# Decoder step with paged attention: keys turned on VectorE in 32x32 blocks, scores in four row bands, two tokens of a page in each partition

## Chip, cores and metric

One Trainium2 chip, one core. The metric is the device time of one execution in microseconds (us), lower is better.

## What is computed

One step of a one-layer decoder for a prompt of 256 tokens and 8 sample sequences of 8 new tokens each: feed-forward, mixer (paged attention and a gated linear state, side by side), feed-forward, each with a conditioned scale, shift and gate. All is fp32. The part around the change is the attention of the sample sequences over their paged past of 2048 tokens, 16 pages of 128 tokens, 8 heads of 64:

```python
k_past = cache_k[layer, page_table].reshape(B, past, H, HD)
kmean = jnp.mean(k_past[:, :own0].reshape(B, n_full, MOBA_BLOCK, H, HD), axis=2)
idx, ok = moba_select(q, kmean, n_full)          # top 3 of 8 blocks of 256 tokens, per query and head
...
s_sel = jnp.einsum('bqhd,bhqnkd->bqhnk', q, k_sel) * scale
s_sel = jnp.where(ok[..., None], s_sel, -jnp.inf).reshape(B, H, T, -1)
...
o = sparse_softmax_attend(s_sel, v_sel, s_own, v_own)
```

## The kernel before

The activations stand as [128 partitions = channel, 8 channel tiles, 320 tokens]: 256 prompt and 64 sample columns. Weights stream through four raw slots of 8 KB a partition; ScalarE rounds each to a high part (`wh`), VectorE subtracts for the low part (`wl`), and TensorE makes three products (L691, L692, L696). The slots are numbered: conditioning and first feed-forward, the mixer's input projection MI (74 to 85), its output projection MO (86 to 89), second feed-forward.

**The page stage** lies between MI and MO. The 8 sequences are taken as 4 pairs `i`, with `bi` the member of the pair. A page is 256 KB in K and as much in V; four pages make a group of 1 MB, so there are 32 K groups and 32 V groups. Each is loaded by `load_pages` on SyncE's queue: four DMAs of one page, token per partition, 2 KB a packet (L619), in the written order `PAGE_GROUPS`. `place_groups` gives each group a buffer: four in `ring` (over the raw slots), and for parts of the stage places in `Hh`/`Hl`, in `M` and in `W`. SyncE waits with each group until the last user of its buffer is done (`wait_used`).

For each K group `turn_keys(i, j, bi)` makes 16 transposes on TensorE (L887), one PSUM bank of four for each page; ScalarE (`keys_act`) or VectorE (`keys_dve`, L1785) copies each bank to `kT`. `scores(i, j)` (L898) then multiplies for both members and four head pairs `c`: stationary `Qz` (128 x 32, zeros where another head stands), moving 512 tokens of `kT`, each product in its own 32 columns of the array, so that four lie side by side, in bank `B[j % 2]`. VectorE reduces the bank twice, sum for the choice of blocks and maximum (`block_values`, L1792 and L1794), ScalarE copies it to `prob` (`scores_out`).

After four `j` VectorE's `choose` (L1812 to L1823) ranks the blocks and makes the biases; ScalarE takes the exps (`exps`), TensorE turns the probabilities (`turn_probs`, L918), both engines copy them to `PT`, and `values(i, bi)` (L936, own tokens L941) multiplies with V as it landed, in PSUM bank 2. `own_heads` (VectorE, L1849), `pick_heads` (TensorE, L950), `out_high` and `out_low` move the result to the input of MO.

**What sets the order.** Every engine's order is written out by hand. Between these steps stand the mixing steps `mix(k)`, placed by `point(x)` and the table `AT_POINT`: 0 to 6 are the prompt's own attention (per head on VectorE L1864 to L1877), 12 to 15 the output and norm of the gated linear part (L1011 to L1035), 16 to 19 the new sample states (TensorE L1053, VectorE L1965). What TensorE fills in PSUM in this stage (turned keys, mixing results, own scores, turned probabilities, picked heads) rotates over banks 3 to 7 in the written order `FILLS`; `turn_bank` waits until the engine that reads the bank's former content is done. Engines run each its own list in order, so whatever waits holds all that stands behind it.

`turn_keys` and `scores` of before:

```python
for p in range(4):
    bank = turn_bank(("k", i, j, bi, p))
    for c in range(HP):
        m = pe.transpose(bank[:, c * P:(c + 1) * P], at[p][:, c * P:(c + 1) * P], ident)
```
```python
m = pe.matmul(B[j % 2][32 * c:32 * c + 32, :], Qz[:, 2 * i + bi, c, :], kT[:, bi, c, :],
              start=(bi == 0), stop=(bi == 1))
```

Of the kernel before, what the change touches and what calls it, by code (L numbers as in the profile page):

```python
# [21 lines left out]
F32 = mybir.dt.float32  # L22
# [38 lines left out]
GROUPS = RING // 4  # L61
# [76 lines left out]
def key_fills(i, j):  # L138

    return [("k", i, j, bi, p) for bi in range(2) for p in range(4)]  # L140


PAGE_GROUPS = [("k", 0, j, bi) for j in range(4) for bi in range(2)]
# [6 lines left out]
for _lv in range(6):  # L150
    GAPS[6 + _lv] += mix_fills(7 + _lv)
GAPS[8] += [("nv", t) for t in range(3)]
# [3 lines left out]
AT_POINT = {0: 0, 1: 1, 3: 2, 4: 3, 5: 4, 6: 5, 8: 6, 9: 12, 10: 13, 11: 14, 13: 15, 14: 16, 15: 17, 16: 18, 18: 19}  # L156
# [5 lines left out]


FILLS += key_fills(0, 0) + key_fills(0, 1) + point_fills(0) + key_fills(0, 2) + point_fills(1) + [("own", 0)]
FILLS += key_fills(0, 3) + point_fills(2)
for _i in range(NPAIR):
    _m = 5 * _i + 3
    if _i + 1 < NPAIR:
        PAGE_GROUPS += [("k", _i + 1, j, bi) for j in range(2) for bi in range(2)]
        FILLS += key_fills(_i + 1, 0) + point_fills(_m) + key_fills(_i + 1, 1) + point_fills(_m + 1)  # L170
    else:
        FILLS += point_fills(_m)
    PAGE_GROUPS += [("v", _i, g, 0) for g in range(4)]
    if _i + 1 < NPAIR:
        PAGE_GROUPS += [("k", _i + 1, 2, bi) for bi in range(2)]
    PAGE_GROUPS += [("v", _i, g, 1) for g in range(4)]
    FILLS += [("p", _i, q) for q in range(5)]
    if _i + 1 < NPAIR:
        PAGE_GROUPS += [("k", _i + 1, 3, bi) for bi in range(2)]
        FILLS += point_fills(_m + 2) + key_fills(_i + 1, 2) + point_fills(_m + 3) + [("own", _i + 1)]  # L180
        FILLS += key_fills(_i + 1, 3) + point_fills(_m + 4) + [("pick", _i)]
    else:
        FILLS += point_fills(_m + 1) + [("pick", _i)]
GROUP_AT = {key: n for n, key in enumerate(PAGE_GROUPS)}
FILL_AT = {key: n for n, key in enumerate(FILLS)}
IN_RING, IN_H, IN_M, IN_W = range(GROUPS), GROUPS, GROUPS + 1, GROUPS + 2
BEGIN_AT = {GROUP_AT[("v", 1, 0, 0)]: IN_M, GROUP_AT[("v", 2, 0, 0)]: IN_W}
LAST_IN = {IN_H: GROUP_AT[("v", 2, 3, 0)], IN_M: GROUP_AT[("k", 3, 3, 1)], IN_W: GROUP_AT[("v", 3, 0, 0)]}


def place_groups():

    queue, last, buf, before = [(MI + x) % R for x in range(R)] + [IN_H], {}, [], []
    for n in range(len(PAGE_GROUPS)):
        if n in BEGIN_AT:
            queue.insert(0, BEGIN_AT[n])
        queue = [b for b in queue if n <= LAST_IN.get(b, n)]
        b = queue.pop(0)
        queue.append(b)
        buf.append(b)  # L200
        before.append(last.get(b))
        last[b] = n
    return buf, before, last
# [4 lines left out]
BANK = [4 + n % 4 if n < IN_MI else 3 + (n - IN_MI) % 5 for n in range(len(FILLS))]  # L208
# [3 lines left out]
def on_act(key):  # L212

    if key[0] == "k":
        _, i, j, bi, p = key
        if j == 0:
            return i == 0 or p != 3
        return p % 2 == 0 if j >= 2 else (bi == 1 and p % 2 == 1)
    if key[0] == "p":
        return key[2] in (2, 3)  # L220
    if key[0] == "ga":
        return key[1] == 5
    return key[0] in ("rg", "nk", "nv", "nvg", "pt", "kd", "sp")
# [17 lines left out]
def shape_constants():  # L241
# [24 lines left out]
    parts["cos"], parts["sin"] = cos, sin  # L266
    q = p[:, None]
# [16 lines left out]
    reset = np.ones((P, N))  # L284
    reset[:, [0] + [S + T * b for b in range(NB)]] = 0.0
    parts["reset"] = reset
# [26 lines left out]
def layer_kernel(nc, a, o):  # L313
    ctx = ExitStack()
    with ctx:
# [17 lines left out]
        ring = sb("ring", [P, RING, 512])  # L333
        kT = sb("kT", [P, 2, HP, 512])
# [24 lines left out]
        Qz = sb("Qz", [P, NB, HP, 32])  # L359
# [20 lines left out]
        B = [ctx.enter_context(nc.psum_tensor(f"B{i}", [P, 512], F32)) for i in range(8)]  # L380
        OB = 2
# [13 lines left out]
        def raw_view(n):  # L395

            if n == MO:
                return M[:, :, :].rearrange("p c n -> p (c n)")[:, 0:SLOT]
            return W[:, 0:SLOT] if n == MO + 1 else raw[:, n % R, :]
# [5 lines left out]
        def page_at(b, j):  # L405
# [4 lines left out]
            if b == IN_M:  # L410
                return M[:, :, :].rearrange("p c n -> p (c n)")[:, 512 * j:512 * j + 512]
            if b == IN_W:
                return W[:, 512 * j:512 * j + 512]
            return ring[:, 4 * b + j, :]

# [42 lines left out]
        gmask = C("gmask").rearrange("p (l i) -> p l i", l=5)  # L458

# [3 lines left out]
        page_landed = [sem(f"page_landed_{i}") for i in range(GROUPS + 3)]  # L463
# [26 lines left out]
        tp_filled, tp_act, tp_dve = sem("tp_filled"), sem("tp_act"), sem("tp_dve")  # L490
        s_out, own_ready, bias_ready, exp_done = sem("s_out"), sem("own_ready"), sem("bias_ready"), sem("exp_done")
        rinv_ready, v_used, pv_out, om_ready = sem("rinv_ready"), sem("v_used"), sem("pv_out"), sem("om_ready")
        o_hi, s_act, s_dve = sem("o_hi"), sem("s_act"), sem("s_dve")
# [184 lines left out]
        def _(pe):  # L678
# [211 lines left out]
            def scores(i, j):  # L890

                if 4 * i + j >= 2:
                    pe.wait_ge(s_act, 4 * i + j - 1)
# [1376 lines left out]
```

## Time and profile before

| | |
|---|---|
| median of 3 runs | 982.14 us (980.75 to 983.33) |
| profiled execution, its own time | 983.45 us |
| its span, first to last instruction | 981.3 us |
| TensorE matmul busy | 919.1 us (94%), 6991 instructions |
| TensorE weight load busy (beside the matmuls) | 798.8 us |
| VectorE, ScalarE, GpSimd busy | 545.9, 359.5, 28.1 us |
| HBM read | 195.00 MB, 203 GB/s over the span |
| chain that ended last | TensorE 83%, VectorE 6%, ScalarE 3%, SyncE's queue 3% |

The profile is one execution. "Busy" is the time in which an engine had an instruction in work; for TensorE the trace keeps two records for each fp32 product and one for a transpose. The page's second part cuts the span in 40 slices of 24.5 us. PEclk is the granted TensorE clock as a share of 2.4 GHz, and the DMA share is the mean busy share of the core's 16 DMA engines, which can read a little over 1 where packets overlap.

### The profile page before, as it was taken

To read this page: it belongs to the slowest core of one execution; us is meant where nothing else is said; L and a number is where in the kernel's file an instruction comes from. 1 tells how busy PE (TensorE), PEld (TensorE's weight loads), DVE (VectorE), ACT (ScalarE), POOL (GpSimd) and SP (SyncE) were. 2 spreads that over 40 slices of the span, in tenths; PEclk is the share of its full clock that TensorE was granted. 3 is DMA by queue.
4 is the path that set the end of the run, shared out by engine and by line. 5 is a ranking of instruction groups with operands and counts; after the bars stand their busy time and mean duration, and the time that the engine had idled before them with its cause. 6 is when DMAs were issued, how large, how long until landed. Compare 5 with 4: busy or idle time off the path is not lost.

```text
span 981.3 us, 17319 instructions
## 1 busy us (share of the span) xinstructions
PE 919.1 (94%) x6991; PEld 798.8 (81%) x6991; DVE 545.9 (56%) x839; ACT 359.5 (37%) x509; POOL 28.1 (3%) x34
## 2 busy tenths in 40 slices
PE   6999999999999899999878999859899999989997
PEld 2588888988999599996665877548779999989994
DVE  0545444454655677785843538443666765554655
ACT  1424322232442534454642426240333232323433
POOL 0000000000000000000000000001200000000000
PEclk9999999998999999999999889877999999999999
DMA  9899889886456744448858998996416465534511
GB/s 329 258 299 258 240 244 257 245 235 169 127 152 191 256 129 145 144 153 268 297 190 325 324 325 310 356 343 199 125 39 167 133 163 139 145 89 122 155 50 53
DMA packets 214885, 199.93 MB, mean 204 GB/s; under 512 B 9569, under 2 KB 161261, under 8 KB 214678
## 3 DMA queue, kind: packets, MB, share of 16 engines
q1 hardware_dynamic: 213412, 194.99, 64.8%
q0 software_dynamic: 704, 2.49, 0.7%
q10 hardware_dynamic: 690, 1.35, 0.4%
q8 instruction: 55, 0.90, 0.4%
q14 instruction: 24, 0.20, 0.1%
HBM read 195.00 MB, written 3.80 MB: 203 GB/s over the span
## 4 chain that ended last, share of the span: by engine, by line
PE 83%; DVE 6%; ACT 3%; SPq 3%; issue 2%; DMA 2%; ACTq 0%; DVEq 0%
PE B L691 20%; PE B L692 19%; PE B L696 19%; PE B L751 4%; PE B L887 3%; PE B L898 2%; SPq L619 2%; PE B L936 2%; PE B L775 2%; PE B L760 2%; PE B L791 2%; DMA ring<-in_cache_v 1%; PE B L1017 1%; PE B L717 1%; PE B L712 1%
## 5 line engine op out<-in xcount | busy, mean ns | idle before, releaser
L691 PE MATMUL B<-Hh,wh 128*128 128x320 f32 x912 | 274.2, 314 | 0.6 <-issue 0.6
L692 PE MATMUL B<-Hl,wh 128*128 128x320 f32 x912 | 270.5, 310 | 0.0
L1595 DVE TENSOR_TENSOR wl<-raw,wh 128x2048 fp32r<-128x2048 f32 x90 | 207.3, 2305 | 94.3 <-ACT wh L1240 94.0
L1240 ACT ACTIVATE wh<-raw 128x2048 fp32r<-128x2048 f32 x90 | 172.3, 1914 | 150.3 <-PE B L696 117.6
L691 PEld LDWEIGHTS B<-Hh,wh 128*128 128x128 f32 x912 | 172.4, 189 | 10.7 <-issue 10.0
L692 PEld LDWEIGHTS B<-Hl,wh 128*128 128x128 f32 x912 | 172.4, 189 | 0.3
L696 PE MATMUL B<-Hh,wl 128*128 128x320 f32 x912 | 152.8, 310 | 0.0
L696 PEld LDWEIGHTS B<-Hh,wl 128*128 128x128 f32 x912 | 139.1, 189 | 0.0
L691 PE MATMUL B<-Gh,wh 128*128 128x320 f32 x352 | 107.1, 317 | 2.5 <-DVE Gl L1721 2.5
L692 PE MATMUL B<-Gl,wh 128*128 128x320 f32 x352 | 106.7, 316 | 0.0
L1240 ACT ACTIVATE sg<-B 128x320 f32<-128x320 f32 x46 | 20.1, 438 | 210.1 <-PE B L696 195.7
L1713 DVE TENSOR_TENSOR hf<-sg,B 128x320 f32<-128x320 f32 x44 | 21.5, 488 | 124.6 <-ACT sg L1240 124.6
L691 PEld LDWEIGHTS B<-Gh,wh 128*128 128x128 f32 x352 | 68.5, 195 | 2.7 <-DVE Gl L1721 2.7
L692 PEld LDWEIGHTS B<-Gl,wh 128*128 128x128 f32 x352 | 68.6, 195 | 0.0
L887 PE MATMUL B<-cst,ring 128*128 128x128 f32 x432 | 53.2, 277 | 7.0 <-DVE kT L1785 1.8
L887 PEld LDWEIGHTS B<-cst,ring 128*128 128x128 f32 x432 | 47.1, 141 | 14.4 <-issue 6.4
L696 PE MATMUL B<-Gh,wl 128*128 128x320 f32 x352 | 56.8, 309 | 0.0
L696 PEld LDWEIGHTS B<-Gh,wl 128*128 128x128 f32 x352 | 53.1, 188 | 0.0
L1785 DVE COPY kT<-B 128x512 f32<-128x512 f32 x62 | 40.2, 686 | 21.9 <-PE B L887 21.5
L1240 ACT ACTIVATE kT<-B 128x512 f32<-128x512 f32 x66 | 36.0, 611 | 24.4 <-PE B L887 24.3
L936 PE MATMUL B<-ring,PT 128*32 128x128 f32 x672 | 26.0, 308 | 14.3 <-DMA ring<-in_cache_v 14.3
L751 PE MATMUL B<-raw,cpk 128*32 128x512 f32 x288 | 38.8, 617 | 0.3 <-ACT cpk L1240 0.3
(246 smaller groups left out, 951.8 us busy)
## 6 DMA issues: line engine op xcount, KB each, us to landing
raw<-in_w_ffn_in SPq DMA_DIRECT2D x88, 512.0 KB, 6.2
raw<-in_w_ada SPq DMA_DIRECT2D x72, 512.0 KB, 4.9
ring<-in_cache_k SPq DMA_DIRECT2D x108, 256.0 KB, 5.3
ring<-in_cache_v SPq DMA_DIRECT2D x84, 256.0 KB, 5.0
raw<-in_w_ffn_out SPq DMA_DIRECT2D x32, 384.0 KB, 3.6
raw<-in_w_mix_in SPq DMA_DIRECT2D x24, 512.0 KB, 4.7
raw<-in_w_ffn_out SPq DMA_DIRECT2D x32, 320.0 KB, 4.3
M<-in_cache_v SPq DMA_DIRECT2D x16, 256.0 KB, 4.5
```

The source lines that it names most:

```text
L619: sp.dma_start(page_at(b, j), cache[bass.ds(page[j], 1), :, :].rearrange("o s f -> s (o f)")).then_inc(page_landed[b], 16)
L691: pe.matmul(out, w, xh[k], start=start and k == 0, stop=False)
L692: pe.matmul(out, w, xl[k], start=False, stop=False)
L696: m = pe.matmul(out, w, xh[k], start=False, stop=stop and k == last)
L751: m = pe.matmul(B[4 + pair % 2][32 * k:32 * k + 32, :], cpk[:, 4 * half + k, :], v[:, k, :], start=(half == 0), stop=(half == 1))
L760: m = pe.matmul(B[bank][:, col:col + NC], arow[:, h // 2, h % 2 * P:(h % 2 + 1) * P], C("comb"), start=True, stop=True)
L887: m = pe.transpose(bank[:, c * P:(c + 1) * P], at[p][:, c * P:(c + 1) * P], ident)
L936: m = pe.matmul(out[32 * c:32 * c + 32, :], PT[:, 4 * g + p, 32 * c:32 * c + 32], at[p][:, c * P:(c + 1) * P], start=(g == 0 and p == 0), ...
L1240: return act.activation(out, in_, func, **kw)
L1595: dve.tensor_tensor(wl[:, wbuf(n), :], raw_view(n), f32(wh[:, wbuf(n), :]), ALU.subtract).then_inc(lo_ready, 1)
L1713: step(dve.tensor_tensor(hf[:, j, :], sg[:, j, :], B[2 * j][:, 0:N], ALU.mult))
L1785: dve.tensor_copy(kT[:, bi, :, p * P:(p + 1) * P], tb(key).rearrange("p (c s) -> p c s", c=HP)).then_inc(tp_dve, 1)
```

## The change

- K pages are turned on VectorE: one in-place `transpose` for a group, 128 x 2048, which turns each 32x32 block within itself. `kT`, the key transposes and the key copies go.
- A page lands two tokens to a partition (64 partitions, 4 KB a packet), K and V alike; two pages fill 128 partitions. Each page is still one DMA.
- Scores take the turned blocks in four bands of 32 rows (`a`): a chunk is two K groups of one member (8 pages) and 64 products of 32 rows, 32 columns and 256 moving columns; 16 chunks in all. The four bands write four PSUM banks, `S4` (over banks 0 to 3).
- The queries are turned to fit (`turn_queries`, 8 calls of 16 products), ScalarE copies them to `Qs`.
- ScalarE copies a band set in 4 pieces and sums each block on the way (`accum_out`); VectorE takes only the maximum (`block_max`), from `prob` in SBUF.
- Six ring groups of 1 MB instead of four, and other late places; value products use bank 4; the fills rotate over banks 5 to 7 instead of 3 to 7. `Qz` lies over constants that are dead by then and is cleared later, after the rotary step.
- Mixing steps move to other points; the turned probabilities' first quarter is copied by ScalarE.

The diff, cut to its core:

```diff
-GROUPS = RING // 4
+GROUPS = 6
...
+AT_POINT = {x: x if x <= 6 else x + 5 for x in range(15)}
...
+USE = [key for s in range(2) for bi in range(2) for key in key_groups(0, s, bi)]
+FILLS += point_fills(0) + point_fills(1) + [("own", 0), ("q", 1, 0)] + point_fills(2) + [("q", 1, 1)]
+    for _x in range(3):
+        FILLS += point_fills(4 * _i + 3 + _x)
+    FILLS += [("p", _i, q) for q in range(5)] + point_fills(4 * _i + 6)
+        USE += key_groups(_i + 1, 0, 0) + key_groups(_i + 1, 0, 1) + value_groups(_i, 0)
+        USE += key_groups(_i + 1, 1, 0) + value_groups(_i, 1) + key_groups(_i + 1, 1, 1)
+        FILLS += [("q", _i + 2, 0)] if _i + 2 < NPAIR else []
+        FILLS += [("own", _i + 1)]
+        FILLS += [("q", _i + 2, 1)] if _i + 2 < NPAIR else []
+        USE += value_groups(_i, 0) + value_groups(_i, 1)
+    FILLS += [("pick", _i)]
+PAGE_GROUPS = [key for key in USE if key != ("v", 0, 0, 0)]
+PAGE_GROUPS.insert(6, ("v", 0, 0, 0))
...
-BANK = [4 + n % 4 if n < IN_MI else 3 + (n - IN_MI) % 5 for n in range(len(FILLS))]
+BANK = [4 + n % 4 if n < IN_MI else 5 + (n - IN_MI) % 3 for n in range(len(FILLS))]
...
-                    sp.dma_start(page_at(b, j), cache[bass.ds(page[j], 1), :, :].rearrange("o s f -> s (o f)")
+                    sp.dma_start(page_pair_at(b, j // 2)[64 * (j % 2):64 * (j % 2) + 64, :],
+                                 cache[bass.ds(page[j], 1), :, :].rearrange("o (s x) f -> s (o x f)", x=2)
                                  ).then_inc(page_landed[b], 16)
...
+            def turn_queries(i, bi):
+
+                bank = turn_bank(("q", i, bi))
+                if i == 0:
+                    pe.wait_ge(q_ready, 4)
+                for x in range(4):
+                    for q in range(4):
+                        m = pe.matmul(bank[32 * q:32 * q + 32, P * x:P * (x + 1)], ident[:, 32 * x:32 * x + 32],
+                                      Qz[:, 2 * i + bi, :, :].rearrange("p c r -> p (c r)"), start=True, stop=True)
+                m.then_inc(tp_filled, 1)
+
+            def scores(i, s, bi):
+
+                if bi == 0 and 2 * i + s >= 1:
+                    pe.wait_ge(s_act, 2 * i + s)
+                if s == 0:
+                    wait_act(("q", i, bi))
+                pe.wait_ge(k_turned, 2 * chunk(i, s, bi) + 2)
+                b = BUF[GROUP_AT[("k", i, 2 * s, bi)]]
+                for x in range(4):
+                    for a in range(4):
+                        for c in range(HP):
+                            f = P * c + 32 * x
+                            m = pe.matmul(S4[32 * c:32 * c + 32, a, 0:256].rearrange("r (p j) -> r p j", p=8),
+                                          Qs[32 * a:32 * a + 32, bi, x, c, :],
+                                          ring[32 * a:32 * a + 32, 4 * b:4 * b + 8, f:f + 32],
+                                          start=(bi == 0 and x == 0), stop=(bi == 1 and x == 3))
+                m.then_inc(s_out, 1)
...
+            scores(0, 0, 0)
             point(0)
+            scores(0, 0, 1)
             point(1)
             own_scores(0)
+            scores(0, 1, 0)
+            turn_queries(1, 0)
             point(2)
+            scores(0, 1, 1)
+            turn_queries(1, 1)
             for i in range(NPAIR):
+                m0 = 4 * i + 3
                 if i + 1 < NPAIR:
                     point(m0)
+                    scores(i + 1, 0, 0)
                     point(m0 + 1)
+                    scores(i + 1, 0, 1)
+                    point(m0 + 2)
                     turn_probs(i)
                     values(i, 0)
                     point(m0 + 3)
+                    scores(i + 1, 1, 0)
+                    if i + 2 < NPAIR:
+                        turn_queries(i + 2, 0)
                     values(i, 1)
                     own_scores(i + 1)
+                    scores(i + 1, 1, 1)
+                    if i + 2 < NPAIR:
+                        turn_queries(i + 2, 1)
                     pick_heads(i)
                 else:
                     turn_probs(i)
                     values(i, 0)
                     values(i, 1)
                     pick_heads(i)
...
+            def queries_out(i, bi):
+
+                wait_fill(("q", i, bi))
+                if i >= 1:
+                    act.wait_ge(s_out, chunk(i - 1, 1, bi) + 1)
+                act_(Qs[:, bi, :, :, :].rearrange("p x c r -> p (x c r)"), tb(("q", i, bi))).then_inc(tp_act, 1)
+
+            def scores_out(i, s):
+
+                act.wait_ge(s_out, chunk(i, s, 1) + 1)
                 if i >= 1:
                     wait_fill(("p", i - 1, 4))
+                for m in range(4):
+                    n = 4 * s + m
+                    last = act_(prob[:, BLK * n:BLK * (n + 1)].rearrange("p (a j x) -> p a x j", a=4, x=2),
+                                S4[:, :, 64 * m:64 * m + 64].rearrange("p a (x j) -> p a x j", x=2),
+                                accum_out=gate[:, n:n + 1])
+                last.then_inc(s_act, 1)
...
+            def turn_keys(i, s, bi):
+
+                for g in (2 * s, 2 * s + 1):
+                    n = GROUP_AT[("k", i, g, bi)]
+                    b = BUF[n]
+                    dve.wait_ge(page_landed[b], 64 * TURN_IN[n])
+                    v = ring[:, 4 * b:4 * b + 4, :].rearrange("p j f -> p (j f)")
+                    dve.transpose(out=v, in_=v).then_inc(k_turned, 1)
+
+            def block_max(i, s):
+
+                dve.wait_ge(s_act, 2 * i + s + 1)
+                dve.tensor_reduce(bmax[:, 4 * s:4 * s + 4],
+                                  prob[:, 4 * BLK * s:4 * BLK * (s + 1)].rearrange("p (n k) -> p n k", n=4), X_AXIS,
+                                  ALU.max).then_inc(dve_step, 1)
                 step.k += 1
...
+                if n >= 10:
+                    turn_keys(0, 0, n - 10)
 
             def point(x):
                 if x in AT_POINT:
                     mix(AT_POINT[x])
 
             point(0)
+            turn_keys(0, 1, 0)
             point(1)
+            block_max(0, 0)
             own(0)
+            turn_keys(0, 1, 1)
             point(2)
             for i in range(NPAIR):
+                m0 = 4 * i + 3
+                block_max(i, 1)
+                choose(i)
                 if i >= 1:
                     out_low(i - 1)
                 if i + 1 < NPAIR:
+                    turn_keys(i + 1, 0, 0)
                     point(m0)
+                    turn_keys(i + 1, 0, 1)
                     point(m0 + 1)
+                    point(m0 + 2)
+                    totals(i)
                     probs_dve(i, 1)
+                    probs_dve(i, 4)
+                    point(m0 + 3)
+                    block_max(i + 1, 0)
+                    turn_keys(i + 1, 1, 0)
+                    own_heads(i)
+                    own(i + 1)
+                    turn_keys(i + 1, 1, 1)
+                else:
                     totals(i)
+                    probs_dve(i, 1)
                     probs_dve(i, 4)
                     low(At(MO))
                     own_heads(i)
                     out_low(i)
```

## Rows read from the trace of the kernel before

**Rows 1.** The page, second part: rate in each of 40 slices.

```profile
GB/s 329 258 299 258 240 244 257 245 235 169 127 152 191 256 129 145 144 153 268 297 190 325 324 325 310 356 343 199 125 39 167 133 163 139 145 89 122 155 50 53
```

**Rows 2.** Windows: length, PE, PEld, DVE, ACT, POOL busy, PEclk, DMA share, GB/s.

```profile
482.00:533.00 51.00, 39.09 (x526) 28.90 (x519) 25.68 (x67) 20.02 (x60) 0.00 (x0) 0.93 0.77 270
533.00:588.00 55.00, 53.73 (x622) 44.17 (x621) 25.26 (x55) 19.84 (x49) 0.00 (x0) 0.88 0.88 305
...
638.00:670.00 32.00, 19.25 (x305) 15.11 (x305) 12.07 (x31) 10.18 (x25) 1.18 (x1) 0.66 0.95 320
sum 223.00, PE 188.53 PEld 142.62 DVE 118.09 ACT 93.35 POOL 1.90; mean PE 37.71 PEld 28.52 DVE 23.62 ACT 18.67 POOL 0.38
```

**Rows 3.** Groups by form, 447 to 670 us: busy, mean ns | idle before, releaser.

```profile
L887 PE MATMUL B<-cst,ring 128*128 128x128 f32 x432 | 53.2, 277 | 7.0 <-DVE kT L1785 1.8 <-DMA ring<-in_cache_k 1.7 <-DVE arow L1801 1.6
...
L1785 DVE COPY kT<-B 128x512 f32<-128x512 f32 x62 | 40.2, 686 | 21.9 <-PE B L887 21.5
...
L898 PE MATMUL B<-kT,Qz 128*32 128x512 f32 x256 | 33.7, 640 | 0.1
...
L1240 ACT ACTIVATE prob<-prob,small 128x256 f32<-128x256 f32 x32 | 15.9, 507 | 4.0 <-DVE small L1823 4.0
L1792 DVE TENSOR_REDUCE small<-B 128x2 f32<-128x512 f32 x16 | 11.0, 688 | 43.4 <-PE B L898 43.4
```

**Rows 4.** Waits of SyncE's DMA queue: total us, times, longest.

```profile
SPq L619 <- PE B L936: 33.6, 5, 10.8
```

**Rows 5.** Timeline and L906's source view, TensorE: start, us, records.

```profile
464.90 1.92 PE L898 MATMUL B<-kT,Qz 128*32 128x512 f32 x16
466.64 0.41 PE L906 MATMUL B<-knew,Qz 128*32 128x64 f32 x16
...
574.59 1.94 PE L936 MATMUL B<-M,PT 128*32 128x128 f32 x32
578.23 1.04 PE L936 MATMUL B<-ring,PT 128*32 128x128 f32 x32
...
L906 PE MATMUL B<-knew,Qz x64: 219/219/220, 466.6 to 631.8; 128*32 128x64 f32 x64
```

**Rows 6.** Page, fifth part, and source view of L1902: VectorE within SBUF.

```profile
L1595 DVE TENSOR_TENSOR wl<-raw,wh 128x2048 fp32r<-128x2048 f32 x90 | 207.3, 2305 | 94.3 <-ACT wh L1240 94.0
...
L1902 DVE TENSOR_SCALAR Z<-Z x5: 427/427/428, 400.0 to 435.7; 128x512 f32<-128x512 f32 x5
```

**Rows 7.** Timeline of VectorE: choice of blocks, prompt mixing, state update.

```profile
479.66 0.21 DVE L1812 TENSOR_TENSOR small<-small 128x64 f32<-128x64 f32 x1
...
482.00 0.56 DVE L1864 TENSOR_TENSOR Z<-B,cst 128x384 f32<-128x384 f32 x1
...
485.95 3.67 DVE L1785 COPY kT<-B 128x512 f32<-128x512 f32 x6
...
601.73 1.23 DVE L1965 SCALAR_TENSOR_TENSOR W<-W,rstd,B 64x128 f32<-64x128 f32 x4
```

**Rows 8.** Timeline of TensorE: first rows of mixing 13, values, mixing 14.

```profile
548.24 0.46 PE L1011 MATMUL B<-W 128*128 128x128 f32 x2 [1.11 <-issue]
...
555.14 1.93 PE L936 MATMUL B<-M,PT 128*32 128x128 f32 x32
...
564.69 0.39 PE L1011 MATMUL B<-W 128*128 128x128 f32 x2
```

**Rows 9.** Windows of one microsecond, columns as in rows 2.

```profile
522.00:523.00 1.00, 1.00 (x28) 0.99 (x24) 0.00 (x0) 0.00 (x0) 0.00 (x0) 0.53 1.05 389
16.00:17.00 1.00, 1.00 (x7) 0.24 (x9) 0.00 (x0) 0.00 (x0) 0.00 (x0) 1.00 1.06 422
```

**Rows 10.** Timeline of the stage's end: last choice, values, output projection.

```profile
642.18 0.23 DVE L1823 TENSOR_SCALAR small<-small 128x8 f32<-128x8 f32 x1
...
647.87 1.29 PE L936 MATMUL B<-W,PT 128*32 128x128 f32 x32
...
670.02 0.61 PE L691 MATMUL B<-Hh,wh 128*128 128x320 f32 x1 [0.62 <-issue]
```

## Prediction before the run

> **What bounds the kernel now.** The change touches one stage, so I first read the rates by fortieths of the span, to find it: from slice 18 on the rate stands near 325 GB/s for ten slices and falls to 39 right after [rows 1]. Those are the 64 MB of K and V pages. The windows of that stage then say who fills it. Of 223 us TensorE is busy 188.5, VectorE 118.1 and ScalarE 93.4, and even the transfers' share falls to 0.77 in one stretch [rows 2]. Nothing is saturated throughout: TensorE leads from 533 to 588 us, and from 638 to 670 us it is busy only 19 of 32. The costliest groups show what TensorE does for the keys: 432 of the 512 transposes on ring tiles take 53.2 us, the scores 33.7 us, and VectorE copies the turned keys out of PSUM for 40.2 us, with reductions of 11 us each for sum and maximum [rows 3]. Last, SyncE's own waits: it stood 33.6 us for the value products to free a buffer before it could issue the next pages [rows 4]. So the bound alternates: TensorE's instructions, then pages issued late because the ring was full.
>
> **What the change removes.** (a) TensorE's 512 key transposes. Sixteen take about 1.92 us in a stream, so 61 us. (b) The old scores, 16 calls of 1.92 us [rows 5], less the overlap at their ends: 28 us. (c) On VectorE 62 key copies (40.2 us) and 32 reductions out of PSUM (22 us) [rows 3]. (d) The key copies on ScalarE, which has room [rows 2]; its new copies of the scores (four pieces of 256 columns, 2.2 us by the 0.5 us that one exp of 256 columns takes here [rows 3]) are shorter than what they replace.
>
> **What it adds.** (e) VectorE turns 32 key groups of 128x2048 in place. No transpose stands in the trace. From above, four copies of 512 columns out of PSUM would be 2.7 us, and the subtraction of the same 128x2048 takes 2.305 us with two inputs. From below, a one-input instruction of 512 elements within SBUF took 0.427 us; four of them are 1.7 us, and nearly half of each is a fixed part (an instruction of 64 elements takes 0.21), so 0.43 + 3 x 0.25 = 1.2 us for 2048 [rows 3, 6, 7]. I take 2.2 us, near the subtraction, because that is the row of the same size and a transpose is no plain pass; 4.4 us for the two groups that one score chunk needs, 70 us in all.
> (f) Scores in bands: 16 chunks of 64 fp32 products (32 rows, 32 columns, 256 moving), which the trace counts twice each, as it does the old ones: 128 records. The row nearest in kind is the own-key score, 16 records of 64 moving columns in 0.41 us, of which 0.22 is the length of one: 13 ns apart [rows 5]. With four times the columns but four times as many products side by side the array needs the same 13 ns: 1.9 us a chunk. That is the lower bound. A long stream, the value products, held 27.5 ns a record (32 in 0.88 and the latency) [rows 5]: 3.7 us. If the four bands do not run beside one another, four records share 0.215 us (half of the 0.43 us of the 512-column ones): 7.0 us. At the lower clock level, 1.2 GHz, the array's own times double: the first bound becomes 3.6 us. The clock follows how full TensorE is: mean 0.88 where it was busy 53.7 of 55 us, 0.66 where it was busy 19.3 of 32, and 0.53 at 522 us, so practically the lower level, behind a wait for pages [rows 2, 9]; 32 value records then take 1.94 us, at full clock 1.04 [rows 5]. Most chunks will start behind 4 to 5 us of waiting for VectorE's turning, so I take 3.6 us.
> A rule of the Trainium skill speaks against the change here: "TensorEngine Tiling (Array Packing)", section Performance Considerations, has about 60 cycles of overhead in each matmul. By it a chunk would need 3.2 us at full clock and 6.4 at half, and the sum would end 28 us later. The own-key row, at 13 ns a record, does not show that overhead, so its case is a rival (R4) and not the forecast.
> (g) The queries are turned in 8 calls of 32 records, at 27.5 ns 0.9 us each. Two sit in the projection loop, where TensorE is never idle: 1.8 us straight onto the path.
> (h) Packets of 4 KB instead of 2 KB. The page stream peaks near 388 GB/s; in the one microsecond where the 4 KB rows of x_prompt arrive the rate is 422 [rows 9]. Worth at most 8% of a transfer that only matters where it is waited for. I cost it at nothing in the middle: pages wait for buffers there. The DMA count and SyncE's issue work do not change.
> (i) More buffers (six ring groups, three more late): the last pages need no longer wait for values. Today the last choice of blocks ends at 642.4 us, the values start 5.4 us later and wait for pages, and the output projection starts at 670.0 [rows 10]: 27.6 us. With the pages landed these remain: 5.4 us, values of 4.9 us (32 records at the low clock) and 3.7, and 2.4 of head picking, 16.4 us. This is the surest gain, 11 us.
>
> **The path.** The order on VectorE is written out by hand, and a turn waits behind what stands ahead of it. The turn for the third chunk of each pair stands behind the mixing step that follows the first values; the one for the fourth stands behind own_heads, which waits for the second values. So turning is not hidden: turn, scores, values, turn, scores come one after the other. Before, TensorE could turn keys while anything else was late. I follow it from row durations: choice of blocks 2.3 us (479.66 to 482.00), a prompt mixing step on VectorE 4.0 (482.00 to 485.95), two sample-state updates with their masks 3.2 (1.23 for one's four instructions) [rows 7], copy of scores 2.2 plus a maximum of 1.2; mixing step 13 on TensorE 6.9 (548.24 to 555.14) and 14 9.9 (564.69 to 574.59) [rows 5, 8], with 6.5 taken for the first since its opening gap of issue goes.
> Pair 0, from 447.0 us: turns 13.2, mixing, maximum and own keys 8.5, scores 3.6, copy, maximum and choice 5.7: choice 0 ends at 478 us (today 482.0).
> Pair 1: turns 4 x 4.4, scores 3 x 3.6 (one is hidden), mixing 3 and 6 with maxima 7.3, mixing 5 and turned probabilities 3.5, queries 0.9, values 2 x 3.9, own heads 1.1, copy and choice 5.7: 54.8, choice 1 at 532.8.
> Pair 2: turns 3 x 4.4 (one lies beside mixing 13), scores 4 x 3.6, mixing 13 to 15 19.0, probabilities 2, values 4.9 and 4.2, maximum, queries, own heads, remainders 3.7, copy and choice 5.7: 67.1, choice 2 at 599.9.
> Pair 3: turns 4 x 4.4, updates 3.2, 4.7 and 3.2, probabilities and values behind them 4.2, mixing 19 with maximum 6.3, scores 2 x 3.6, values 4.2, own heads and rest 1.3, copy and choice 5.7: 57.6, choice 3 at 657.5 (today 642.4).
> Tail 16.4: 673.9. Plus the 1.8 us of (g): the output projection starts at 675.7, today at 670.0. That is 5.7 us more. Behind it nothing changes. The profiled execution took 983.45 us (span 981.3), 1.3 above the median of the runs, 982.14; 983.45 and 5.7 make 989.2, on the median's scale **988 us**. A measurement of this kernel tells 0.3%, some 3 us, from no change. The terms that decide are 14 exposed pairs of turns (62 us) and 10 exposed chunks (36 us), 98 together, against the 89 us of transposes and scores that TensorE loses; the 11 us of (i) stand on the other side.
>
> **Rivals.** R1, scores are quick: TensorE stays at 2.4 GHz and 13 ns a record hold, chunk 1.9 us. For it: the own-key row. Against it: the idle time ahead of the chunks. 10 x 1.7 off: 971. Chance 0.22.
> R2, VectorE turns at its faster one-input rate, 1.2 us a group. For it the 0.427 us row, against it that such a turn crosses partitions. 28 x 1.0 off: 960. Chance 0.07.
> R3, the transfers alone set the end, as the larger packets intend. 60 groups and two weight slots, 65 MB, remain at 446.7; at 388 to 422 GB/s they are in by 614 to 601, and the projection starts 4 us later: 917 to 930. It needs TensorE and VectorE hidden behind them, and TensorE alone needs 188 - 89 + 52 + 6 = 157 us. Chance 0.05.
> R4, slower beyond my forecast: the bands bring no more than four products side by side, because their row groups do not overlap or because each record has a floor of its own. Place: each chunk. Price: 7.0 us, or the 54 ns a record of the values at the low clock, 6.9, against 3.6: 10 x 3.4 = 34, so 1022. It turns a tie into a loss from about 4 us a chunk on. Chance 0.13. The skill's 60 cycles above would end here as well.
> R5, a turn costs twice my value, 4.4 us a group: 28 x 2.2 = 62: 1050. Chance 0.05.
> R6, the change does not free TensorE as it says: three rotating PSUM banks instead of five make it wait for copies. Two of the five probability fills a pair then wait for a copy of 0.69 us and its hop of 0.2: 4 x 2 x 0.9 = 7 us, 995. Chance 0.08.
>
> **How the numbers follow.** The forecast has 0.40, with 978 to 998 as its own spread (ten hops of 0.2 us a pair that I did not count push up, warm chunks push down). Faster by over 0.3%: R1 to R3, 0.34, and 0.03 of the forecast's own spread: 0.37. Same, 979.2 to 985.1: 0.15 of that spread. Slower: the rest, 0.48. Range 955 to 1018: it leaves out R3, the near-zero end of R2, R5 and the far half of R4, some 0.2.
>
> **What would show it.** Right: transposes near 2.2 us on VectorE with TensorE idle ahead of each chunk, released by VectorE; chunk times near 3.6 us at clock 0.5; values no longer waiting for pages; choice 1 earlier than today, choice 3 later. Wrong: chunks under 2.5 us; transposes under 1.5; a page stream at 400 GB/s without gaps, which would mean that the chain of turns was hidden after all.

## The result and the profile after

The changed kernel took 1075.88 us (median, 1071.58 to 1078.92), the kernel before 981.44 us on the same chip (978.08 to 983.33): 1.096 times as long, 95% interval 1.091 to 1.102. Forecast were 988 us and a range of 955 to 1018. The sign of the forecast stands, its size doesn't: 94 us were lost, not 6. The profiled execution took 1078.92 us (span 1076.8). Medians and intervals here are of runs in the faster of the chip's two states, which leaves out two of four runs of e3 and one each of e6 and e10 below; the traces of e3 and e10 are of such slower runs.

The page of the kernel after, second and third parts (compare the rates with [rows 1]):

```profile
PEclk9999999989999999977666777566789999999998
DMA  9898898874567345796999899999751555533521
GB/s 333 251 307 252 239 249 239 238 199 115 155 216 250 109 154 136 166 250 166 213 224 241 188 217 206 224 212 237 199 137 40 154 143 144 146 108 108 161 56 49
...
q1 hardware_dynamic: 197028, 194.99, 68.6%
```

Three windows of the kernel after (length, PE, PEld, DVE, ACT, POOL busy, PEclk, DMA share, GB/s):

```profile
450.00:470.00 20.00, 12.58 (x356) 7.08 (x347) 16.53 (x30) 4.72 (x17) 0.00 (x0) 0.75 1.04 232
510.00:530.00 20.00, 10.47 (x231) 8.62 (x231) 6.94 (x6) 3.65 (x13) 0.00 (x0) 0.70 1.05 229
710.00:730.00 20.00, 6.89 (x139) 4.76 (x140) 8.07 (x14) 4.38 (x20) 0.00 (x0) 0.65 1.06 242
```

Read the last two columns together. The DMA engines are full (1.04 to 1.06) and move 229 to 242 GB/s. The kernel before moved 389 with engines just as full [rows 9]. The transfers themselves have become slow: from issue to landing a page of keys for the ring takes 7.6 us (median), before 5.3, and a page of values 11.0, before 5.0. The stage now ends at 764.05 us, before at 670.0 [rows 10], so practically the whole loss lies in it.

Groups of the kernel after, 447 to 766 us (busy, mean ns | idle before, releaser), the transposes from the page, then waits of SyncE's queue and of TensorE in the same stretch:

```profile
L940 PE MATMUL S<-ring,Qs 32*32 32x256 f32 x2048 | 70.8, 573 | 85.5 <-DVE ring L1805 62.5 <-issue 21.6 <-DVE M L2080 1.4
L1810 DVE TENSOR_REDUCE small<-prob 128x4 f32<-128x1024 f32 x8 | 9.7, 1214 | 24.5 <-ACT prob L1277 24.5
```

```profile
L1805 DVE STREAM_TRANSPOSE ring<-ring 128x2048 f32<-128x2048 f32 x32 | 72.4, 2292 | 11.8 <-DMA ring<-in_cache_k 11.7
```

```profile
SPq L654 <- PE S L940: 91.0, 13, 17.2
```

```profile
PE S L940 <- DVE ring L1805: 62.5, 11, 9.8
PE S L940 <- issue: 21.6, 7, 4.8
PE B L984 <- DMA ring<-in_cache_v: 12.3, 3, 7.6
```

A turn takes 2.29 us. TensorE stands 62.5 us for turns; the forecast's 62 were 14 waits of 4.4, these are 11, some of them with a late page of keys in them, so that the two sums agree is in part luck. SyncE's queue stands 91.0 us for score products (L940), because keys stay in the ring until they are scored. Before, it stood 33.6 us for values [rows 4] and little for keys:

```profile
SPq L619 <- PE B L887: 12.6, 8, 2.4
```

Chunks and tail, timeline of TensorE after:

```profile
504.89 2.75 PE L940 MATMUL S<-ring,Qs 32*32 32x256 f32 x128 [2.22 <-DVE ring L1805]
568.63 4.31 PE L940 MATMUL S<-ring,Qs 32*32 32x256 f32 x128 [8.31 <-DVE ring L1805]
...
746.32 1.94 PE L984 MATMUL B<-ring,PT 128*32 128x128 f32 x32 [7.55 <-DMA ring<-in_cache_v]
...
764.05 0.60 PE L727 MATMUL B<-Hh,wh 128*128 128x320 f32 x1 [0.62 <-issue]
```

These two chunks take 2.75 us, behind a wait of 2.2 (granted clock 1.00, the level of 2.4 GHz), and 4.31 behind one of 8.3 (0.54, close to the level of 1.2 GHz). The last choice ends at 727.3 us, and 37 us pass to the output projection, since the last values wait for pages.

### The profile page after: what moved, and what is told of

It reads as the page before. It is cut to its first block, busy times and chain, and to the rows that moved or that the text cites. A ratio compares the mean times of both kernels' runs of the same rounds, so it can differ in the third digit from the quotient of the medians.

```text
span 1076.8 us, 20151 instructions
## 1 busy us (share of the span) xinstructions
PE 920.8 (86%) x8527; PEld 798.6 (74%) x8527; DVE 565.7 (53%) x781; ACT 335.0 (31%) x503; POOL 28.0 (3%) x34
## 3 DMA queue, kind: packets, MB, share of 16 engines
q1 hardware_dynamic: 197028, 194.99, 68.6%
## 4 chain that ended last, share of the span: by engine, by line
PE 77%; DVE 10%; issue 5%; DMA 4%; SPq 2%; ACT 2%; ACTq 0%; DVEq 0%
PE B L727 18%; PE B L728 17%; PE B L732 17%; PE S L940 5%; DVE ring L1805 5%; PE B L787 3%; SPq L654 2%; PE B L984 2%; PE B L811 2%; PE B L827 2%; PE B L796 2%; DMA ring<-in_cache_v 2%; DMA ring<-in_cache_k 2%; PE B L1065 1%; DVE small L1810 1%
## 5 line engine op out<-in xcount | busy, mean ns | idle before, releaser
L940 PE MATMUL S<-ring,Qs 32*32 32x256 f32 x2048 | 70.8, 573 | 85.5 <-DVE ring L1805 62.5
L940 PEld LDWEIGHTS S<-ring,Qs 32*32 32x32 f32 x2048 | 41.8, 130 | 107.3 <-issue 72.4
L1805 DVE STREAM_TRANSPOSE ring<-ring 128x2048 f32<-128x2048 f32 x32 | 72.4, 2292 | 11.8 <-DMA ring<-in_cache_k 11.7
L1277 ACT ACTIVATE prob<-S 128x256 f32<-128x256 f32 x32 | 12.1, 412 | 103.9 <-PE S L940 103.9
```

The lines of the kernel that those rows point to most:

```text
L940: m = pe.matmul(S4[32 * c:32 * c + 32, a, 0:256].rearrange("r (p j) -> r p j", p=8), Qs[32 * a:32 * a + 32, bi, x, c, :], ring[32 * a:32 * ...
L1277: return act.activation(out, in_, func, **kw)
L1805: dve.transpose(out=v, in_=v).then_inc(k_turned, 1)
```

## The experiments

The theories were: **T1**, a transfer that lands on half of the partitions is slow; **T2**, rows of 4 KB are slow; **T3**, the engines stretch the stage and the stream follows. A softmax does not mind the order of its keys, so keys and values of a block may lie on any partitions, if both lie alike. That makes the layout free to vary.

### Where a page lands

e1 and e2 alter the changed kernel, e3 and e4 the kernel before:

```diff
-  sp.dma_start(page_pair_at(b, j // 2)[64 * (j % 2):64 * (j % 2) + 64, :], <two tokens a row, 4 KB>)
+  sp.dma_start(page_pair_at(b, j // 2)[:, 512 * (j % 2):512 * (j % 2) + 512], <one token a row, 2 KB>)   # e1
+  sp.dma_start(page_pair_at(b, j // 2)[j % 2::2, :], <two tokens a row, 4 KB>)                           # e2
-  sp.dma_start(page_at(b, j), <one token a row, 2 KB>)
+  sp.dma_start(page_pair_at(b, j // 2)[64 * (j % 2):64 * (j % 2) + 64, :], <two tokens a row>)           # e3
+  sp.dma_start(page_pair_at(b, j // 2)[j % 2::2, :], <two tokens a row>)                                 # e4
```

> The changed kernel with each page again on all 128 partitions in rows of 2 KB; everything else of the change stays (bands, turn on VectorE, order). T1 (a transfer that lands in 64 partitions is slow): the page stream is back near 388 GB/s and the kernel takes 980 to 1000 us, what the forecast's serial path gives. T2 (rows of 4 KB are slow as such): the same. T3 (the work on VectorE and TensorE stretches the stage and the stream only follows): 1060 to 1080 us, stream 230 to 250 GB/s.

> The changed kernel with its rows of 4 KB, but a page's 64 rows go to every second partition of the 128 instead of one half. T1 in the form that a half is slow because it is one contiguous half: as the run with 2 KB rows, 980 to 1000 us. T1 in the form that 64 rows are too few: 1060 to 1080 us. T2: 1060 to 1080 us. T3: 1060 to 1080 us.

> The kernel before with the changed kernel's page transfers alone: two tokens of a page in each partition, a page in 64 partitions, rows of 4 KB. T1 and T2: the stream falls to 230 to 250 GB/s with nothing else changed, and the kernel takes 1050 to 1090 us. T3: 975 to 990 us, as before.

> The kernel before with rows of 4 KB on every second partition. T1 (contiguous half): 960 to 985 us, at most a little faster than before. T1 (too few rows) and T2: 1050 to 1090 us. T3: 975 to 990 us.

Measured, against 980.34 us for the kernel before: e1 1019.21 (ratio 1.035 to 1.044), e2 1017.85 (1.034 to 1.044), e3 1016.94 (1.030 to 1.045, mean of 1011.83 and 1022.05; all four runs scatter up to 1038.52), e4 979.66 (0.997 to 1.003). e4 came in as T1's narrow form expects. e1 and e2 lie between their expectations, and e3 between 990 and 1050: the layout costs time in both kernels, but less than its theory said. The stretch 520 to 535 us of e3, and the same slices of the pages of e3 and e4:

```profile
520.00:535.00 15.00, 6.73 (x108) 4.92 (x112) 0.00 (x0) 0.00 (x0) 0.00 (x0) 0.57 1.05 229
...
GB/s 332 258 298 248 244 244 244 243 206 154 154 179 275 131 126 149 144 210 247 215 229 236 239 260 272 258 270 224 189 90 82 150 138 160 151 89 119 156 57 51
```

```profile
GB/s 327 259 300 257 239 252 253 244 232 181 120 149 201 258 129 131 155 156 261 291 167 339 305 325 345 299 357 251 128 50 166 132 167 134 145 89 124 157 47 54
```

e3 has not one transpose on VectorE, and for these 15 us VectorE and ScalarE do nothing at all; its engines still read 1.05 at 229 GB/s. So it is not the work of VectorE and ScalarE that slows the stream. e4 has the same 197,028 packets of 4 KB and streams at the old rate. T1 stands in its narrow form: neighbouring partitions, not few rows or long ones. T2 and T3 fall as causes of the slow stream. The changed kernel lies 94 us over the kernel before of its own chip, e2 38, so the layout costs some 57 us here; in the kernel before it costs 37 (31 and 42 in the two runs). Some 38 us remain, for which T3's kind of cause is needed.

### Turn, clock and chunk

All on e2, which from here on is the base. e5 moves the turns on VectorE, e6 leaves all but 32 columns of each out, e7 fills TensorE's waits, e8 and e12 leave half of the score products out:

```diff
+  turn_keys(i + 1, 0, 0)          # e5, ahead of block_max(i, 1) and choose(i)
   block_max(i, 1); choose(i)
-  turn_keys(i + 1, 0, 0)
+  turn_keys(i + 1, 0, 1)
   point(m0)
-  turn_keys(i + 1, 0, 1)
   ...
+  turn_keys(i + 1, 1, 0)
   point(m0 + 3); block_max(i + 1, 0)
-  turn_keys(i + 1, 1, 0)
+  turn_keys(i + 1, 1, 1)
   own_heads(i); own(i + 1)
-  turn_keys(i + 1, 1, 1)
```

```diff
-  dve.transpose(out=v, in_=v)                                    # e6
+  dve.transpose(out=v[:, 0:32], in_=v[:, 0:32])
+  for _ in range(10): pe.matmul(<free columns>, ident, ident)    # e7, before nine chunks
   pe.wait_ge(k_turned, 2 * chunk(i, s, bi) + 2)
-  for x in range(4):                                             # e8, e12
+  for x in range(2):
```

> The changed kernel with 4 KB rows on every second partition (1018 us) and VectorE's order altered: the turns of each of the next pair's four chunks stand one place earlier, ahead of the maxima, the copy of the own columns or the heads they stood behind. Ta (what is left over before is the turn standing in line before each chunk, 60.9 us of TensorE's idle time): 990 to 1005 us. Tb (TensorE's low clock stretches the chunks): 1010 to 1020 us. Tc (the buffers of K, held until the scores, starve the stream in the middle, and its last 40 pages come after the last chunk): 1005 to 1015 us, since an earlier turn frees a buffer earlier.

> The same kernel with the turn on VectorE left out but for 32 columns of each group (32 turns of 2.29 us go, the scores are of unturned keys). Ta: all that the stage lost and more comes back, 955 to 980 us. Tb: 1000 to 1015 us. Tc: 975 to 995 us, where the stream becomes the limit.

> The same kernel with ten idle products of 128x128 on TensorE before nine of the sixteen chunks, in the time in which it waits for the turn (2.2 us at the full clock, results unused). Tb (chunks of 4.3 us at the half clock against 2.75): the granted clock of the stage rises from 0.75 to over 0.85 and 10 to 20 us come back, 998 to 1008 us. Ta and Tc: 1012 to 1025 us.

> The same kernel with half of each chunk's score products left out (64 of 128; two of the four quarters of a head's rows). If the chunk's length is what is exposed (16 of 4.2 us, of which half goes, and half of the stalls named issue): 985 to 995 us. If only the turn is (Ta alone): 1005 to 1015 us.

> Every second partition, the turns early (994.6 us) and the ten idle products before nine chunks (alone 9 us of gain) together. If the two gains add, 984 to 988 us, still not under the kernel before. If the idle products filled just the wait that the early turns have since removed, 993 to 998 us.

> The changed kernel as it is (pages on halves of the partitions, 1076 us) with the early turns alone. If the slow stream sets the stage, the early turns are worth less here than the 23 us that they gave with the full stream: 1062 to 1076 us. If turn and stream cost independently of each other: 1050 to 1056 us.

> Every second partition, the turns early (994.6 us), and half of each chunk's score products left out. If the 15 us that are left over before are the length of the chunks on TensorE: 976 to 984 us. If they are the stream, which starts late because a page of keys holds its buffer until it is scored: 984 to 992 us, since a shorter chunk frees the buffer sooner by 1.3 to 2 us only.

| | us | ratio to before, 95% | us over before, same chip | from | of its expectations |
|---|---|---|---|---|---|
| e5 turns early | 994.60 | 1.012 to 1.021 | 15.8 | e2 1017.85 (37.5 over) | Ta |
| e6 no turns | 984.61 | 1.001 to 1.009 | 5.8 | e2 | Tc |
| e7 idle products | 1008.96 | 1.025 to 1.041 | 30.1 | e2 | just over Tb |
| e8 half of the products | 1002.95 | 1.021 to 1.031 | 24.1 | e2 | between the two |
| e9 = e5 + e7 | 1004.01 | 1.017 to 1.027 | 21.9 | e5 | neither, 6 us over the higher |
| e11 after + e5's order | 1052.73 | 1.068 to 1.080 | 70.6 | after 1075.88 (94.4 over) | independent |
| e12 = e5 + e8 | 986.49 | 1.004 to 1.009 | 4.7 | e5 | the stream |

The runs were made on several chips, so a difference between two kernels is best read from the fourth column.

Groups of e2 (440 to 710 us), then of e5 (440 to 700):

```profile
L940 PE MATMUL S<-ring,Qs 32*32 32x256 f32 x2048 | 66.9, 553 | 66.7 <-DVE ring L1805 60.9 <-issue 4.3 <-DVE M L2080 1.4
```

```profile
L1805 DVE STREAM_TRANSPOSE ring<-ring 128x2048 f32<-128x2048 f32 x32 | 72.7, 2296 | 38.0 <-DMA ring<-in_cache_k 37.9
L940 PE MATMUL S<-ring,Qs 32*32 32x256 f32 x2048 | 60.3, 500 | 28.7 <-DVE ring L1805 23.8 <-issue 3.2 <-DVE M L2080 1.4
```

The order alone gives 22 us on the good layout and 24 on the bad one, so layout and order cost independently of each other. TensorE's wait for turns falls from 60.9 to 23.8 us, but VectorE now waits 37.9 us for pages of keys. Without the turns at all 32 us come back, not 60. That the stream is next fits e5; in e6 it is not shown, since VectorE waits only 9.5 us for keys there and TensorE still 22.9 for what is left of L1805. Half of the products give 13 us, and 11 once the order is mended: the chunks' length is on the path in both.

The idle products do what they are for and bring nothing that can be told. In the stretch 447 to 670 us the granted clock is 0.76 in e2, 0.82 in e7, 0.77 in e5 and 0.83 in e9, and nine of the twelve chunks of pairs 1 to 3 take 2.76 us in e9, three in e5. Yet e7 is 7 us better than e2 and e9 is 6 us worse than e5, and in both pairs the intervals overlap. The expected sum of two gains (984 to 988) did not come. A cold clock is thus not a large term by itself; that the idle products are work on the path in e9 is argued, not shown.

### The last 16 us

e13 and e14 issue keys ahead of the values (i, 1), one chunk or two; e15 moves the third piece of mixing of each pair behind the first values on TensorE, VectorE and ScalarE. All are on e5.

```diff
+  for _key in key_groups(_i + 1, 1, 1) [+ key_groups(_i + 2, 0, 0)]:    # e13 [e14]
+      ISSUE.remove(_key); ISSUE.insert(ISSUE.index(("v", _i, 0, 1)), _key)
-  point(m0 + 2)                                                        # e15
   turn_probs(i); values(i, 0)
+  point(m0 + 2)
   point(m0 + 3)
```

> Every second partition, the turns early (994.6 us, in which VectorE waits 37.9 us for pages of keys), and SyncE's order altered: the last chunk of keys of the next pair is issued ahead of the values (i, 1) instead of behind them. If what is left over before is that keys stand in the queue behind values whose buffers are not free: VectorE's wait for keys falls under 20 us and the kernel takes 980 to 989 us. If the stream's total is short anyway, the values come as much later: 992 to 998 us.

> The same with the first chunk of keys of the pair after next issued ahead of those values too. If the queue order is the cause and the keys are still late: 975 to 985 us. If values are then what TensorE waits for: 990 to 1005 us.

> Every second partition, the turns early (994.6 us), and in each pair but the last the third piece of mixing (at 557 to 568 us for pair 1) moved behind the first values, on TensorE, VectorE and ScalarE alike. If what is left over before is the stream standing still from 552 to 579 us (186 GB/s in 550 to 580, where the kernel before moves 316) because no buffer comes free while TensorE mixes: the stretch 550 to 580 rises over 250 GB/s and the kernel takes 982 to 989 us. If the time is in TensorE's and VectorE's serial chain: 993 to 998 us.

Measured: e13 998.67 us (1.013 to 1.022), e14 1010.07 (1.027 to 1.033), e15 991.01 (1.006 to 1.014), e5 having 1.012 to 1.021. All three fall between or beyond their expectations. Windows of the kernel before, of e5 and of e15:

```profile
550.00:580.00 30.00, 30.00 (x405) 27.27 (x408) 5.95 (x10) 5.98 (x12) 0.00 (x0) 0.77 0.91 316
```

```profile
550.00:580.00 30.00, 30.00 (x443) 25.44 (x452) 10.84 (x16) 6.10 (x18) 0.03 (x1) 0.71 0.55 186
```

```profile
550.00:580.00 30.00, 30.00 (x528) 24.93 (x532) 14.16 (x18) 6.11 (x18) 0.72 (x1) 0.78 0.76 259
```

Keys sooner only means values later: in e13 VectorE's wait for keys falls from 37.9 to 11.8 us, as foreseen, but TensorE waits 20.0 us for value pages, in e5 3.4, and the time does not move; e14 is slower still. The queue's order is not the cause. While TensorE mixes, the kernel before goes on streaming at 316 GB/s into buffers that its copies have emptied; in the changed kernel keys and values sit in the ring until they are used, and the rate is 186. e15 brings it to 259, over the 250 foreseen, but the kernel is only 3.6 us faster by the medians and 7 against the kernel before of the same chip (8.6 us over it, e5 15.8), short of the 982 to 989 expected; the intervals overlap. Shown is that the stream stands still there; that it accounts for the whole rest is not. Some 9 us stay open. No version of the changed kernel beats the kernel before.

### What about a half is slow

e10 is e3 with the pages of a group issued in the order 0, 2, 1, 3 (two to the lower half, then two to the upper). e16 and e17 put a page on 32 partitions of the kernel before in rows of 8 KB (but for the groups in `Hh`/`Hl`, which land in e4's way). With four tokens in a partition the blocks of keys are mixed with one another, so the choice of blocks is another; the amount of work is the same.

```diff
-  for j in range(4):
+  for j in (0, 2, 1, 3):                         # e10
-  page_at(b, j)                                 # e16, e17
+  page_four_at(b)[32 * j:32 * j + 32, :]         # e16
+  page_four_at(b)[j::4, :]                       # e17
```

> The kernel before with the changed kernel's page transfers (1029 us), but within a group the two pages of the lower half of the partitions are issued first, then the two of the upper half. If neighbouring transfers overlap and a half is slow only where two in a row write the same half: slower, 1040 to 1070 us. If one transfer writes at a time in the main, whatever comes next: 1025 to 1033 us.

> The kernel before with a page on 32 neighbouring partitions in rows of 8 KB, four tokens in each (but for the groups that land in the tiles of the activations; blocks of keys are then mixed with one another, so the choice of blocks is another, and the amount of work the same). If the rate goes with how many of the partitions a transfer covers in one stretch: a page stream of 110 to 150 GB/s and 1150 to 1250 us. If the half was a special case: 1020 to 1050 us.

> The same with a page on every fourth partition, rows of 8 KB. If only the spread over the partitions counts, not how many rows or how long: 975 to 985 us, as before. If 32 rows are too few for sixteen engines: 1030 us and more.

Measured: e10 1047.89 us (ratio 1.059 to 1.071), e16 1048.23 (1.049 to 1.085, two runs), e17 978.94 (0.994 to 1.003, the kernel before of that chip at 982.30). Windows of e16, then of e17:

```profile
520.00:535.00 15.00, 7.60 (x116) 4.77 (x120) 0.00 (x0) 0.00 (x0) 0.00 (x0) 0.66 1.02 219
535.00:550.00 15.00, 10.52 (x92) 6.82 (x84) 6.84 (x13) 4.95 (x10) 0.00 (x0) 0.89 1.03 234
```

```profile
520.00:535.00 15.00, 14.84 (x162) 10.68 (x156) 7.09 (x14) 6.10 (x13) 0.00 (x0) 0.91 0.95 330
```

Every fourth partition is as good as all of them, so the count of rows does not matter. A quarter in one stretch is not half as fast as a half but about the same (219 to 234 GB/s); the 110 to 150 expected did not come, and the time fits the other expectation, 1020 to 1050. e10 says that what the neighbours do counts too: its runs (1039.4 to 1047.9) lie clear above those of e3 (1011.8 and 1022.1), as its first expectation had it, and from 525 to 600 us its stream moves 219 GB/s where e3's moves 235.

Two readings fit. Engines that work at one time on one stretch of partitions may get in each other's way, and transfers in flight to other stretches relieve this in part. Or the ways into the partitions may be tied to the partition's number, so that 32 neighbours reach no more of them than 64, while every second or fourth partition reaches all. The second would explain at once why half and quarter are alike and why both spread layouts run at the old rate; for e10 something of the first is needed as well. Neither mechanism is shown: no run lands a page on blocks of neighbours taken from both halves, which would separate them.

## Why the prediction was wrong

**(h) failed.** "I cost it at nothing in the middle": the row of x_prompt, 422 GB/s at 4 KB [rows 9], is a row of the right packet size and the wrong shape, since that transfer covers all 128 partitions. I read the change as one of packets and did not look for a row of a transfer that lands on half of the partitions. The trace of before has one: x_sample, issued at 8.26 us right behind x_prompt, is 256 KB in rows of 4 KB onto partitions 0 to 63 (L628). Its issue, then the two microseconds behind the 422 (length, PEclk, DMA share, GB/s):

```profile
xn<-in_x_sample SPq DMA_DIRECT2D x1, 256.0 KB, 11.5
17.00:18.00 1.00, 1.00 1.14 274
18.00:19.00 1.00, 1.00 0.94 195
```

It lands at 19.8 us, and just before that the rate falls to 274 and 195 GB/s with the engines full or nearly so, where the four microseconds before hold 360 to 422 and the one from 20 on 391. One transfer is thin evidence, but it would have put a cost beside the gain; "worth at most 8%" bounded only the gain. The layout cost 57 us (e2 against the changed kernel), more than all other misses together. "Pages wait for buffers there" was wrong as a cover too: on the chain that ended last in the stage of the changed kernel, pages in flight alone are 10.5% of 317 us, and 17 us of it in one piece (742.3 to 759.2) are the last pages of values.

**The path** stood too short by some 30 us: e2, where (h) is mended, took 1018, on the edge of the range. Its choices of blocks tell where: choice 0 ended at 474.7 us (forecast 478), 1 at 540.4 (532.8), 2 at 614.0 (599.9), 3 at 683.8 (657.5). Pairs 1 to 3 were thus given 11, 6 and 12 us too little. Of this, the chunks of (f) are 4.1 to 4.7 us long behind a wait, not 3.6: some 8 us for 11 chunks. The rest was not taken apart; in it are hops, stalls that the profile names issue, and keys that SyncE could issue only at 518.3 us and that were in at 528.6, in the middle of pair 1.

**What held.** (e) A turn took 2.29 us, forecast 2.2; R2 and R5 are out. (f) "Practically the lower level" behind a wait: most chunks behind a long one show it, and warm ones take 2.75 us, 21 ns a record. The four bands do run beside one another: R4's 6.9 us is out. The Trainium skill's 60 cycles for each matmul ("TensorEngine Tiling (Array Packing)", Performance Considerations) are not refuted by this: the forecast's 3.2 and 6.4 us give them to each of the 128 records, but two records are one product (the own-key row's 13 ns a record are 26 a product), and for 64 products the same figure makes an estimate of 1.6 and 3.2 us, which the measured 2.75 and 4.3 do not contradict. That turning is not hidden, the forecast's main argument, held, and with it the sign: without the layout's cost the change still loses 38 us (e2). VectorE's order alone costs 22 to 24 us (e5, e11). (i) The tail fell from 27.6 to 20 us in e2 (choice at 683.8, projection at 703.6; forecast 16.4), and in the changed kernel rose to 37, since the pages were late. R1 is out: 1.9 us a chunk occurred nowhere. R3's full stream occurred in no version.

**Readings that were off.** The rate of the page stage before is not near 325 GB/s for ten slices: [rows 1] has 268 and 297, then 190, then six from 310 to 356, then 199. And "the clock follows how full TensorE is" does not hold as it stands: in the kernel before TensorE had an instruction in work for all of the 30 us from 550 to 580, at a granted clock of 0.77.

**What I overlooked** beside (h): the copies to kT emptied the ring early. By taking them away, the change ties each key buffer to its scores; SyncE's queue then stood 91.0 us for them, 54.2 in e2, where before it stood 12.6 for key transposes. I counted two more ring groups as more buffers and did not count how much longer each is held.

## What to carry to other kernels

Ask of a transfer not only how long its rows are but which partitions it covers: in a stream, put a block of few long rows on every second or fourth partition and not on neighbours; in the kernel before that cost nothing that can be measured (e4, e17), and against neighbours it was worth 37 us there and 57 in the changed kernel. When a copy goes that moved data out of a landing buffer, count how long that buffer is now held, not only what the copy cost. And in an order written by hand, set each operation that another engine waits for at the first place where its input is there, which gave 22 to 24 us.

## What the runs showed of the hardware

- A stream of 256 KB transfers onto 64 or 32 neighbouring partitions kept the DMA engines at 1.02 to 1.06 and moved 219 to 242 GB/s in the windows shown (after, e3, e16). Onto every second or every fourth partition, or all 128, the same pages ran at the old rate (510 to 600 us: before 334 GB/s, e4 325, e17 326, e3 234). Rows of 2, 4 and 8 KB made no difference that can be measured (ratios to the kernel before of e4 0.997 to 1.003, of e17 0.994 to 1.003).
- A transpose in place of fp32 128x2048 on VectorE took 2.29 us, the time of the two-input subtraction of that size (2.30) [rows 6].
- 128 records of products on 32x32 parts of the array took 2.75 us at a granted clock of 1.00 and 4.3 at 0.54.
